# Query latent of a hybrid decoder kernel: three fp32r passes over split raw tokens and split weights, in place of one fp32 product

## The reference, cut to what matters

```python
hn = rms_norm(h, norm_mix[i])                       # h: 272 x 1024
u = hn @ w_in[i]
z, xbc, dt_raw, q_a, kv_a, gate_logits = jnp.split(u, IN_SPLITS, axis=-1)   # q_a: 384 columns, kv_a: 256 + 32
...
q = (rms_norm(q_a, q_norm, MLA_EPS) @ w_uq)         # query latent
kv = (rms_norm(c_kv, kv_norm, MLA_EPS) @ w_ukv)     # key and value latent
...
h = h + (g_ssd * y_ssd + g_mla * y_mla) @ w_out[i]
h = h + moe_ffn(rms_norm(h, norm_ffn[i]), ...)      # 32 experts, top 4
return rms_norm(h, norm_final)[:, N_META:]
```

## Time and profile before

| | |
|---|---|
| median of three runs | 1300.8 us (1300.68 to 1301.29) |
| profiled execution | 1301.11 us |
| its span, first to last instruction | 1299.1 us |
| mean granted TensorE clock | 0.998 |
| PE busy | 1271.6 us, 98% |
| DVE busy | 461.1 us, 35% |
| ACT busy | 348.6 us, 27% |
| HBM read | 465.43 MB, 359 GB/s over the span |

### The profile page before, as it was taken

The page is one execution under the profiler, slowest core; times in us unless marked ns, Lnnn a source line. Parts: engine busy times, 40 slices in busy tenths (PEclk is TensorE's granted clock), DMA queues, the critical chain, the costliest instruction groups (busy, mean ns, idle before and its releaser), DMA issues.

```text
span 1299.1 us, 17685 instructions
## 1 busy us (share of the span) xinstructions
PE 1271.6 (98%) x7139; PEld 646.0 (50%) x7139; DVE 461.1 (35%) x1072; ACT 348.6 (27%) x671; POOL 28.7 (2%) x46
## 2 busy tenths in 40 slices
PE   9999999999999999999999999999999999999997
PEld 7889999999973333333333233333333333323332
DVE  5978889887652112111121111112111112111112
ACT  4667788654441011110110110011110011010102
POOL 1000000022010000000000000000000000000000
PEclk9999999999999999999999999999999999999999
DMA  8332255457889999999999999999999999999996
GB/s 309 128 142 120 97 230 221 170 195 287 318 315 426 420 408 427 429 429 428 430 433 430 430 427 431 431 435 430 431 430 427 431 434 432 430 431 433 424 427 284
DMA packets 32180, 467.24 MB, mean 360 GB/s; under 512 B 4112, under 2 KB 4144, under 8 KB 8704
## 3 DMA queue, kind: packets, MB, share of 16 engines
q1 hardware_dynamic: 31840, 466.00, 85.8%
q10 hardware_dynamic: 288, 0.52, 0.1%
HBM read 465.43 MB, written 1.08 MB: 359 GB/s over the span
## 4 chain that ended last, share of the span: by engine, by line
PE 46%; DMA 23%; DVE 0%; SPq 0%; issue 0%; ACT 0%; DVEq 0%
PE bank L1593 44%; DMA ring<-wts_dram 16%; DMA work<-wts_dram 7%; PE bank L1994 1%; PE bank L2000 1%; PE bank L2024 1%; SPq L433 0%; SPq L567 0%; DVE work L1587 0%; DVE work L1553 0%; ACT work L1004 0%; DVE work L1497 0%; DVE work L1569 0%; DVEq L107 0%; DVE work L1499 0%
## 5 line engine op out<-in xcount | busy, mean ns | idle before, releaser
L1593 PE MATMUL bank<-ring,work 128*64 128x512 f32 (+2 forms) x2168 | 490.0, 586 | 13.1 <-DMA ring<-wts_dram 12.8
L1593 PE MATMUL bank<-work 128*64 128x512 f32 (+8 forms) x2184 | 430.3, 550 | 6.3 <-DMA work<-wts_dram 4.3
L1593 PEld LDWEIGHTS bank<-ring,work 128*64 128x64 f32 (+1 forms) x2168 | 156.4, 138 | 297.3 <-issue 263.9
L1593 PEld LDWEIGHTS bank<-work 128*64 128x64 f32 (+3 forms) x2184 | 148.5, 143 | 258.9 <-issue 239.1
L1593 PE MATMUL bank<-hn_hi,split 128*128 128x256 f32 (+1 forms) x896 | 172.2, 287 | 0.3 <-ACT work L712 0.2
L1520 DVE COPY work<-bank 128x256 f32<-128x256 f32 x30 | 12.7, 425 | 447.3 <-PE bank L2024 447.3
L1593 PEld LDWEIGHTS bank<-hn_hi,split 128*128 128x128 f32 x896 | 141.3, 188 | 1.0 <-ACT work L712 0.4
L1593 PE MATMUL bank<-hn_lo,split 128*128 128x256 f32 (+1 forms) x448 | 127.1, 284 | 0.0
L1100 DVE TENSOR_TENSOR split<-ring,split 128x1024 fp32r<-128x1024 f32 x88 | 109.7, 1248 | 23.1 <-ACT split L673 22.7
L1497 DVE TENSOR_SCALAR work<-bank 128x512 f32<-128x512 f32 x32 | 22.2, 692 | 262.5 <-PE bank L1593 262.5
L931 ACT ACTIVATE work<-bank 128x512 f32<-128x512 f32 x31 | 18.5, 598 | 325.6 <-PE bank L1593 325.6
(11 more groups left out here) (302 smaller groups left out, 939.6 us busy)
## 6 DMA issues: line engine op xcount, KB each, us to landing
ring<-wts_dram SPq DMA_DIRECT2D x83, 2048.0 KB, 19.1
ring<-wts_dram SPq DMA_DIRECT2D x20, 4096.0 KB, 30.3
work<-wts_dram SPq DMA_DIRECT2D x20, 4096.0 KB, 29.3
ring<-slabs_dram SPq DMA_DIRECT2D x23, 2048.0 KB, 8.6
work<-wts_dram SPq DMA_DIRECT2D x23, 2048.0 KB, 14.4
ring<-wts_dram SPq DMA_DIRECT2D x7, 1024.0 KB, 17.7
ring<-decay_rows SPq DMA_DIRECT2D x16, 256.0 KB, 3.4
work<-wts_dram SPq DMA_DIRECT2D x4, 1024.0 KB, 11.4
```

Of the source, the lines that this page charges most:

```text
L1593: return pe.matmul(o, lhsT, rhs, start=start, stop=stop)
```

## The change

The query latent is computed from split operands like the later units. ACT rounds the raw tokens (`raw_hi`, two halves) and the slab `qa` (`qa_w_hi`, two halves); DVE subtracts (`raw_lo`, `qa_w_lo`, the latter in place of the slab). PE does 48 fp32r products of 384 columns where it did 16 in fp32. The slab `qa` is loaded in two halves: the first ahead of the tokens by rows, the second behind them; the vectors follow. DVE no longer runs two chains for the latents' norms but one over five columns, once the query latent has been read; ACT's reads of that latent are placed around the third piece (`hi_of(2)`), and DVE's low parts of the pieces stand at other places in its order. `latent_ready` is now raised behind the key rope.

```diff
@@ sync
+            sp.dma_start(slab("qa")[:, 0:half_qa], qa_dram[:, 0:half_qa]).then_inc(qa_half_in, 16)
             sp.dma_start(xtok[NMETA:P, 0, :], x[0:P - NMETA, :]).then_inc(x_in[0], 16)
             sp.dma_start(xtok[0:NMETA, 0, :], meta).then_inc(x_in[0], 16)
             sp.dma_start(xtok[:, 1, :], x[P - NMETA:2 * P - NMETA, :]).then_inc(x_in[1], 16)
             sp.dma_start(xtok[0:TAIL, 2, :], x[2 * P - NMETA:SEQ, :]).then_inc(x_in[1], 16)
+            sp.dma_start(slab("qa")[:, half_qa:2 * half_qa], qa_dram[:, half_qa:2 * half_qa]).then_inc(slab_in[1], 16)
+            sp.dma_start(vec[:, :], vecs).then_inc(vec_in, 16)
@@ scalar
+            for h in range(2):
+                ks = slice(h * (KD // 2), (h + 1) * (KD // 2))
+                a.wait_ge(hnT_ready, h + 2)
+                a.activation(raw_hi[:, ks, :], hnT[:, ks, :], ACT.Copy).then_inc(front_hi_ready, 1)
+            a.wait_ge(qa_half_in, 16)
+            qa_hi_of(0)
             for b in (0, 2):
...
+            a.wait_ge(*arrived("qa"))
+            qa_hi_of(1)
             a.wait_ge(rsx_ready, 1)
...
-            for p in range(NSPLIT):
+            for p in range(2):
                 hi_of(p)
             a.wait_ge(rsxq_ready, 1)
             for b in range(2):
+                if b:
+                    hi_of(2)
                 a.wait_ge(proj_done, b + 4)
@@ vector
+            d.wait_ge(hnT_ready, 3)
+            front_lo_of(1, raw_lo, hnT, raw_hi, 0)
+            front_lo_of(2, raw_lo, hnT, raw_hi, 1)
+            front_lo_of(3, qa_w_lo, qa_w, qa_w_hi, 0)
             d.wait_ge(consts_ready, 2)
             d.wait_ge(x_in[1], 32)
...
             rstd(rsx, ssx, D, EPS, rsx_ready)
+            front_lo_of(4, qa_w_lo, qa_w, qa_w_hi, 1)
             d.wait_ge(rsx_spread, 1)
...
+            lo_of(2)
+            d.wait_ge(proj_read, 5)
+            d.tensor_scalar(ssk, ssk, 1.0 / KVL, MLA_EPS, ALU.mult, ALU.add)
+            link(d.tensor_scalar(ssq, ssq, 1.0 / QL, MLA_EPS, ALU.mult, ALU.add))
+            rsqrt(sm(11, 5), sm(3, 5), nrt)
+            for b in range(2):
+                d.tensor_scalar(qa[:, b, :], qa[:, b, :], rsq[:, b:b + 1], None, ALU.mult)
+            lo_of(3)
...
-            lo_of(2)
-            d.wait_ge(proj_read, 5)
-            rstd(rsq, ssq, QL, MLA_EPS)
...
             for c in range(4):
-                if c < 3:
-                    lo_of(c + 3)
+                if c < 2:
+                    lo_of(c + 4)
                 conv_of(c)
@@ tensor
-                    last = mm(ps[:, 0:QL], hnT[:, k, NMETA + (b - 1) * P:NMETA + b * P], wsl[:, k, :], k == 0, k == KD - 1)
+                    if b == 1:
+                        pe.wait_ge(front_lo_ready, 3 + k // (KD // 2))
+                    mm(ps[:, 0:QL], raw_hi[:, k, rows], qa_w_hi[:, k, :], k == 0, False)
+                    mm(ps[:, 0:QL], raw_hi[:, k, rows], qa_w_lo[:, k, :], False, False)
+                    last = mm(ps[:, 0:QL], raw_lo[:, k, rows], qa_w_hi[:, k, :], False, k == KD - 1)
```

More of the change, by code:

```diff
@@ L124, in meta_ssd_mla_moe @@
                 end = at + n
+        for name, at, n in [("qa_w_lo", SLOT, KD * QL), ("raw_hi", IN_WORK + 9600, KD * L), ("raw_lo", IN_WORK + 21504, KD * L),
+                            ("qa_w_hi", IN_WORK + 25736, KD * QL)]:
+            with ExitStack() as lent:
+                lent.enter_context(nc.sbuf_tensor(f"before_{name}", [P, at], F32))
+                overlays[name] = lent.enter_context(nc.sbuf_tensor(name, [P, n], F32R))
         ring = sb("ring", NSLOT * SLOT)
@@ L152, in meta_ssd_mla_moe @@
         hn_lo = overlays["hn_lo"][:, :].rearrange("p (k t) -> p k t", k=KD)
+        raw_hi, raw_lo, qa_w_hi, qa_w_lo = (overlays[n][:, :].rearrange("p (k t) -> p k t", k=KD)
+                                            for n in ("raw_hi", "raw_lo", "qa_w_hi", "qa_w_lo"))
         spread = ring[:, 3 * SLOT + 2464:3 * SLOT + 2464 + 3 * 2 * SEQ].rearrange("p (i j t) -> p i j t", i=3, j=2)
@@ L277, in meta_ssd_mla_moe @@
         vec_in, x_in = sem("vec_in"), [sem(f"x_in{b}") for b in range(2)]
-        xT_in, dkv_half_in = [sem(f"xT_in{h}") for h in range(2)], sem("dkv_half_in")
+        xT_in, dkv_half_in, qa_half_in = [sem(f"xT_in{h}") for h in range(2)], sem("dkv_half_in"), sem("qa_half_in")
         slab_in = [sem(f"slab_in{i}") for i in range(3)]
-        hn_hi_ready, hn_lo_ready, hi_ready, lo_ready = sem("hn_hi_ready"), sem("hn_lo_ready"), sem("hi_ready"), sem("lo_ready")
+        front_hi_ready, front_lo_ready, hi_ready, lo_ready = sem("front_hi_ready"), sem("front_lo_ready"), sem("hi_ready"), sem("lo_ready")
         so_half, attn_hi_ready, y2_hi_ready, y2_lo_ready = sem("so_half"), sem("attn_hi_ready"), sem("y2_hi_ready"), sem("y2_lo_ready")
@@ L443, in _ @@
             for i, (name, n) in enumerate(SLABS):
-                if name == "dkv":
+                if name in ("dkv", "qa"):
                     continue
@@ L653, in _, with qa_hi_of @@
             a.activation(spare, small[:, 15:16], ACT.Square)
+            qa_w = slab("qa").rearrange("p (k n) -> p k n", k=KD)
+            def qa_hi_of(h):
+                ks = slice(h * (KD // 2), (h + 1) * (KD // 2))
+                a.activation(qa_w_hi[:, ks, :], qa_w[:, ks, :], ACT.Copy).then_inc(front_hi_ready, 1)
+            for h in range(2):
+                ks = slice(h * (KD // 2), (h + 1) * (KD // 2))
+                a.wait_ge(hnT_ready, h + 2)
+                a.activation(raw_hi[:, ks, :], hnT[:, ks, :], ACT.Copy).then_inc(front_hi_ready, 1)
+            a.wait_ge(qa_half_in, 16)
+            qa_hi_of(0)
             for b in (0, 2):
@@ L665, in hn_hi_of @@
                 a.wait_ge(hnN_ready, i + 1)
-                a.activation(hn_hi[:, 4 * i:4 * i + 4, :], hnN[:, 4 * i:4 * i + 4, :], ACT.Copy).then_inc(hn_hi_ready, 1)
+                a.activation(hn_hi[:, 4 * i:4 * i + 4, :], hnN[:, 4 * i:4 * i + 4, :], ACT.Copy).then_inc(front_hi_ready, 1)
             def hi_of(p):
@@ L1073, in _, with front_lo_of @@
                                 ALU.mult).then_inc(hnT_ready, 1)
+            qa_w = slab("qa").rearrange("p (k n) -> p k n", k=KD)
+            def front_lo_of(n, lo, whole, hi, h):
+                ks = slice(h * (KD // 2), (h + 1) * (KD // 2))
+                d.wait_ge(front_hi_ready, n)
+                d.tensor_tensor(lo[:, ks, :], whole[:, ks, :], hi[:, ks, :], ALU.subtract).then_inc(front_lo_ready, 1)
+            d.wait_ge(hnT_ready, 3)
+            front_lo_of(1, raw_lo, hnT, raw_hi, 0)
+            front_lo_of(2, raw_lo, hnT, raw_hi, 1)
+            front_lo_of(3, qa_w_lo, qa_w, qa_w_hi, 0)
             d.wait_ge(consts_ready, 2)
@@ L1085, in _, with lo_of @@
             for i in range(2):
-                d.wait_ge(hn_hi_ready, i + 1)
-                d.tensor_tensor(hn_lo[:, 4 * i:4 * i + 4, :], hnN[:, 4 * i:4 * i + 4, :], hn_hi[:, 4 * i:4 * i + 4, :],
-                                ALU.subtract).then_inc(hn_lo_ready, 1)
+                front_lo_of(5 + i, hn_lo, hnN, hn_hi, i)
+            def lo_of(p):
+                d.wait_ge(hi_ready, p + 1)
+                d.tensor_tensor(split[p % NSPLIT][:, 1], piece(p), split[p % NSPLIT][:, 0], ALU.subtract).then_inc(lo_ready, 1)
+            for p in range(2):
+                lo_of(p)
             d.wait_ge(vec_in, 16)
@@ L1095, in _ @@
             link(d.tensor_scalar(v("ssd_norm"), v("ssd_norm"), 0.5, None, ALU.mult))
-            def lo_of(p):
-                d.wait_ge(hi_ready, p + 1)
-                d.tensor_tensor(split[p % NSPLIT][:, 1], piece(p), split[p % NSPLIT][:, 0], ALU.subtract).then_inc(lo_ready, 1)
-            for p in range(2):
-                lo_of(p)
-            d.wait_ge(proj_read, 3)
-            rstd(rsk, ssk, KVL, MLA_EPS)
+            lo_of(2)
[6 more added lines that the diff above has]
+            lo_of(3)
             for b in range(NB):
@@ L1119, in _ @@
                 d.tensor_tensor(ckk[:, :, at:at + 16], kr[:, 0], kr[:, 1], ALU.subtract)
-                d.tensor_tensor(ckk[:, :, at + 16:at + ROPE], kr[:, 2], kr[:, 3], ALU.add)
+                last = d.tensor_tensor(ckk[:, :, at + 16:at + ROPE], kr[:, 2], kr[:, 3], ALU.add)
+            last.then_inc(latent_ready, 1)
             dt3 = dtv.rearrange("p (b h) -> p b h", b=NB)
@@ L1124, in _ @@
             d.scalar_tensor_tensor(dta[:, :], dtv[:, :], -1.0, dtv[:, :], ALU.mult, ALU.max).then_inc(dt_abs, 1)
-            lo_of(2)
-            d.wait_ge(proj_read, 5)
-            rstd(rsq, ssq, QL, MLA_EPS)
-            for b in range(2):
-                last = d.tensor_scalar(qa[:, b, :], qa[:, b, :], rsq[:, b:b + 1], None, ALU.mult)
-            last.then_inc(latent_ready, 1)
             def conv_of(c):
@@ L1645, in spread_norms @@
                 mm(bank[7][:, 0:2], shifted[0:NMETA, 0:P], rsx[0:NMETA, 1:3], False, True).then_inc(rsx_spread, 1)
-            wsl = take("qa").rearrange("p (k n) -> p k n", k=KD)
             for b in (1, 2):
                 ps = bank[2 + b]
```

(1 more changed line is left out.)

13 lines of the change are left out of this document (6 added, 7 removed).

## The result

The changed kernel took 1303.28 us in the median of 16 runs (1302.4 to 1305.81), against 1300.85 of 16 runs before (1300.34 to 1301.53): ratio 1.0019, 95% interval 1.0012 to 1.0026. It is slower by 2.4 us, which is still within the 0.2% that the chances counted as no change. The forecast had been 1301.6, its range ended at 1303.0, and the time lies 0.28 above that end.

What follows compares the result with a forecast made beforehand. DVE's chain, not TensorE, was taken to bound the front, whose shift reaches the end. Its terms, 0.3 + 0.4 - 2.2 + 2.3 = +0.8 us, gave 1301.9 profiled and, with the median 0.3 lower, 1301.6; range 1299.3 to 1303.0.

Steps and rivals of the forecast that it cites:

- What bounds the kernel: DVE's gapless chain to `conv_of(7)` sets the third query unit's start (q 2); front shifts reach the end almost one to one.
- Rival 3: Weight stream bound by itself earlier than thought, so the front's +0.8 us is swallowed: 1300.8 us; chance 0.10.
- rival 1: TensorE is the bound and its saving comes through, `cv` 0 and all else 1.35 us earlier: 1299.5 us; chance 0.18.
- The loads: Front loads: half of `qa` ahead delays the tokens' landing by 1.8 us, from 13.35 to 15.15; bounds nothing to 5.0.
- The norm: Tokens' norm: `rsx` at 18.95, TensorE waits 0.35 us for it, and the chain from `rsxq` starts 0.3 later.
- Rival 2: Tokens by rows land later than 15.15, each microsecond moving the chain by one, up to 1304.8 us; chance 0.10.
- the chain from `rsxq`: DVE's chain after the spread of the norm's factors: start at 20.55 to 20.6, +0.3 us.
- The wait for `hn_hi`: DVE waits for ACT's `hn_hi`, with ACT late by 0.45 after reading the `dkv` latents: +0.4 us.
- The one chain: DVE's merged latent norms: one chain of 2.35 us less, one instruction of 0.2 more, -2.2 us.
- a wait on piece 3: DVE before `conv_of(0)`: no wait, since `cv` 0 is done at 31.3 and DVE asks at 33.4.
- The new wait for piece 5: DVE right after `conv_of(0)` idles until ACT has rounded piece 5 at 42.28: +2.3 us.
- The 48 products: TensorE's query latent: 48 fp32r products at 0.175 us, 8.4 instead of 10.1, saving 1.7 us.

Runs made afterwards that it cites:

- e4: Kernel before with one more DVE subtraction of 1088 columns into unread memory ahead of `hn_lo`, a plain delay of 1.2 us; median 1301.92 us.
- e6: Kernel before with two more DVE subtractions into unread memory ahead of `hn_lo`, a plain delay of 2.4 us; median 1303.19 us.
- e1: Changed kernel with DVE's low part of piece 5 back between channels 1 and 2; median 1301.10 us.
- e7: Kernel before with one norm chain, key rope and dt ahead of it, low parts of pieces 3 to 5 where they stood; median 1299.94 us.
- e9: Kernel before with `qa` loaded in halves, both behind the tokens, product in fp32; median 1300.79 us.
- e3: Changed kernel with the two norm chains and piece order of the kernel before; split operands and halved loads stay; median 1302.53 us.
- e5: Kernel before with only the change's order of loads, half of `qa` ahead of the tokens, product in fp32; median 1302.59 us.
- e2: Kernel before with only the single norm chain and the new piece order, loads and fp32 product as before; median 1303.52 us.

## Why the prediction was wrong

The forecast was 1.7 us too low (1301.6 against 1303.28). The profiled execution accounts for 0.6 of it (1302.50, forecast 1301.9). The other 1.1 is the last term: I put the median 0.3 below the profiled execution, as before the change, and it lies 0.8 above.

**What bounds the kernel** held. The front's shift reaches the end one to one (e4, e6, and span less q 2 within 0.3 us in eleven kernels), and DVE's chain, not TensorE, sets q 2: TensorE's saving of 0.64 us at `cv` 0 vanished, and e1 and e7, which only free DVE, moved the end. Rival 3 (swallowed) and rival 1 (TensorE's saving comes through) fall with this.

**The step that failed is the landing of the tokens, in "The loads" and "The norm", and with it the step from the profiled execution to the median.** I took the landing as one number, read from one execution, and added 1.8. Two things are wrong with that.

The first is the base. The execution that I read had early tokens: its squares start at 13.54, the second earliest of seven traces with the loads of before (e9, whose loads differ only behind the tokens, among them), which go from 13.47 to 14.94 with a median of 13.89. The five kernels with half of `qa` ahead go from 15.62 to 16.49, median 15.69. So the half itself took about the 1.8 that I gave it, but on top of a later landing; against my one trace it looks like 2.15.

The second is the room. Before, the norm was done 0.6 to 1.6 us ahead of TensorE's coming to the spread (1.55 in the trace that I read: 17.15 against 18.70), and a late landing vanished in it. DVE's wait of 3.14 us is not this room, since half of it is the spread itself. A delay of 1.8 uses the room up. From then on the landing sets the spread in every trace (3.75 us after the squares, in all six kernels), a late landing goes to q 2 in full, and an early one gives back at most what TensorE waits, 0.65 in the changed kernel. I had worked out a wait of 0.35 there, so the forecast itself said that the room was gone; the median could then no longer be taken from the profiled execution as before.

How a profiled execution lies to its kernel's median fits this. In the seven kernels with the loads of before, the spread starts between 18.17 and 19.16, and the profiled time lies 0.3 below to 0.9 above the median, nearly in the order of the spreads. Of the five kernels with half of `qa` ahead, the four with squares at 15.6 to 15.7 have profiled times 0.2 to 0.8 below their medians, and e3, with squares at 16.49, lies 0.4 above its own. A usual landing with the half ahead would thus be somewhat later than 15.7; this is an estimate from five traces. The slowest runs (1305.81 and 1305.55, over 3 us above the profiled ones) would need a landing later than any trace has. That they are late landings too is not shown: e5 and e9 show that the place of the load causes loss and scatter, but the landing was not measured run by run.

Rival 2 was this mechanism, and its lower end, 1302.7 and on, holds the result; but I had priced it as a fixed lateness with a chance of 0.10, and not as a spread that the change lets through.

**The terms of the sum**, against the changed kernel's trace: the chain from `rsxq` starts at 21.11 and not 20.55 (+0.8 where I had +0.3). The wait for `hn_hi` was +0.1 (start of `hn_lo` less that of `rsxq`: 2.67 against 2.53), not +0.4. The one chain saves about 2.2, as said (the chain that went has 12 instructions, as the prediction counted, and not the 13 of the description): from `hn_lo` to the end of `conv_of(0)` it is 16.64 against 17.29, which is 2.2 less, one piece more (1.14), and 0.40 for a wait on piece 3 that I had called none, since `cv` 0 started at 29.02 and not 28.3. The new wait for piece 5 is 2.20, forecast 2.3; e1 shows it on the path. Sum 0.8 + 0.1 - 2.2 + 0.4 + 2.2 = 1.3, and 1.47 in the trace (61.40 against 59.93). Forecast 0.8.

**The 48 products** take 0.178 each (21.00 to 29.02 for 45). The rows for the form were right (three from 72.46 to 72.99 are 0.177 each; I had put 0.175), and the 162.5 ns that the Trainium skill's formula gives ("TensorE: Matmul & The Clock Gate", Back-to-back issue gap) is below what this case shows.

**The half behind the tokens** cost nothing measurable: e9 has one load more in the queue than the kernel before, and its median is 0.14 lower.

**The range** was too narrow above for a reason that does not lie in the sum: it was made around one profiled execution, although the change used up the very room that had kept late landings from the end.

## What to carry to other kernels

The time between the end of what hangs on a load and the moment when the bottleneck asks for it is also a buffer for the load's spread. Before a transfer is put in front of another one, compare this room (here 0.6 to 1.6 us over seven traces) with the delay (1.8) plus the spread of landings over several traces (1.5), not with the delay alone. Do not take the whole idle time of a waiting engine for the room: 3.14 us of DVE's waiting held only 1.55 of it. Once the room is gone, expect the median to leave the profile.

An operation that is merged to be run once is worth its time only where its last input is early. Here one chain instead of two was worth -2.2 us of work and +4.3 of waits in one order (e2), and 0.9 us less of the whole in another (e7), with the same instructions.

## What the runs showed of the hardware

The same loads in the same order do not land at the same time: over seven traces of kernels whose loads up to the token rows are the same, the squares started 1.5 us apart, 13.47 to 14.94. The issue of the last rows moved by only 0.15 us (4.11 to 4.26); from issue to landing they took 9.1 to 10.5.

TensorE's granted clock fell after some short waits in the expert stream. In the kernel before, 16 products that began after a wait of 1.78 us for weights took 5.26 us; 16 of the same size, 29 us earlier and after a wait of 1.74, took 3.65 at full clock. Timeline, then the stretches of the slow ones (columns as in the earlier trace rows):

```profile
1111.01 3.65 PE L1593 MATMUL bank<-ring,work 128*64 128x512 f32 x16 [1.74 <-DMA ring<-wts_dram]
...
1140.25 5.26 PE L1593 MATMUL bank<-work 128*64 128x512 f32 x16 [1.78 <-DMA work<-wts_dram]
```

```profile
1140.00:1142.00 2.00, 1.75 (x4) 0.53 (x6) 0.00 (x0) 0.00 (x0) 0.00 (x0) 0.53 1.06 459
1142.00:1144.00 2.00, 2.00 (x8) 0.61 (x6) 0.00 (x0) 0.00 (x0) 0.00 (x0) 0.62 0.95 410
```

The clock is granted at half, 1.2 GHz, for most of these 4 us, and at 2.4 GHz after; in the 2 us ahead of the fall TensorE was busy for 0.47. The changed kernel has two such falls, after waits of 1.76 and 1.75 us, and the kernel before has one, and another wait of 1.77 us in it was followed by none: waits of the same length were followed by a fall in some places and not in others. Span less q 2 is the same in both kernels, so 1.6 us of TensorE more or less did not reach the end here, where it waits for weights.
